# A two-block transformer forward pass on one NeuronCore: another order of weight splits, sums and solver steps within the long middle stage

## The chip, the cores and the metric

One NeuronCore of a Trainium2 chip runs the whole program. The metric is device microseconds from start to end of one execution. The engines are called as the profile calls them: PE (TensorE), PEld (its weight loads), DVE (VectorE), ACT (ScalarE), POOL (GpSimd) and SP (SyncE, which only issues DMAs here).

## What is computed

512 tokens of width 1024 go through two blocks in float32. Cut to what matters here:

```python
# first block, after its attention
x = x + merged @ w_o
u = relu(rmsnorm(x, g_mlp) @ w_up)                       # 1024 -> 4096
x = x + (u * u) @ w_down                                 # 4096 -> 1024
x = x + sigmoid(rmsnorm(x, g_ple) @ w_ple_gate) * (p @ w_ple)
x = rmsnorm(x, g_final)
# second block, first layer: gated delta rule
proj = rms_norm(x, pre_mix_norm) @ gdn_w_in              # q, k, v, z, b, a
q, k, v = silu(causal_conv4(proj[qkv]))                  # q and k then L2-normalised
z = proj[z]
# per chunk of tokens and head: a unit lower triangular system is solved
o = gated_delta_rule(q, k, v, g, beta)
x = x + rms_norm((rms_norm(o) * silu(z)) @ gdn_w_out)
```

Feed-forward layers, a forgetting attention and the first block's two attentions stand around this and are not touched.

## The kernel before

**Products.** Activations are kept with features on the partitions, `x[128, 8, 512]`. A float32 product is made of three passes of PE: each operand is split into a high part (rounded to fp32r) and a low part (what is left), and `product` issues high x high, high x low and low x high (lines 422 to 424). A tile of 128 output features over 1024 inputs is 8 steps k of 3 matmuls of 128x128 on 512 columns, 24 matmuls (`whole_tile`).

**Weights.** They come as a sequence of numbered chunks of up to 128x2048 (1 MB), in two slots used in turn. Chunk n is loaded by SP (line 192) once the low part of chunk n-2 is made; ACT writes its high part (`split_high`, line 213) once PE has finished with chunk n-2, since it overwrites that slot; DVE (`split_low_vector`, line 240) or POOL (`split_low`, line 230) then writes the low part, and PE waits for that. For most chunks this is two output tiles, 48 matmuls. Each engine goes through its own list in program order, so a split stands behind all that its engine was given before.

**The long stage.** `gdn_project` opens a stage without a barrier inside. Every engine first runs the parts of `Ahead` (merge, output projection of the attention, MLP, embedding, embedding gate), then its own part of the projection `gdn_in`:

- `Mlp` goes in two halves: 16 tiles up (8 chunks), ReLU on ACT, square on DVE, split; then 8 chunks down into 8 PSUM banks. DVE scales each bank by the norm's factor and adds it to x (`scale`, `add`). The norm's factor is not needed before that: sums of squares (`sum_squares`, line 1202), mean and reciprocal on DVE, `spread_factor` (line 1209) on PE, `copy_factor` (line 1219) on ACT.
- `PleGate`: chunks g0 to g3 of the gate, two tiles each. Per tile t DVE multiplies by the factor (line 1599), ACT takes tanh, DVE gates (line 1607) and adds to x (line 1610); then ACT and DVE split x for the next projection (`first_high`, `first_low`, line 1650) and square and accumulate it (lines 1658, 1668 and, with a gain, 1673). `FinalEntry.sum_squares` (line 1679) waits for all of these.
- The projection: chunk c0 works on the unnormalised split of x, with the sums in between; c1 is a narrow chunk of 16 columns; from c2 on `FinalEntry.operand` has made the normalised `split` (lines 1736 and 1740). The low parts of chunks c1 to c9 are made by POOL, the later ones by DVE. Each of the 24 tiles of q, k and v goes through a convolution: one tap and tanh on ACT (lines 2305, 2312), three taps on DVE from PSUM (line 2468), a product (line 2475). PE may reuse a bank when the taps have read it (`bank_free`).
- Side computations run beside it: masks and decays, and for the solver the blocks of a triangular matrix go out to DRAM and back as M and X (line 2176). `solve(j)`, 31 steps of two DVE instructions each (lines 2400, 2403), forms the inverse in X; it is copied transposed (line 2509) and both are written out.
- The gates z: two sides of 512 columns, two chunks each (z0 to z3). PE needs the banks read by DVE (line 2487) before the next side; line 2492 makes `z2`. In the kernel before, five solver steps follow each of the eight gate tiles.

The stage ends in a barrier of all engines (line 150), behind which `gdn_chain` starts at line 2579.

Of the kernel before, what the change touches and what calls it, by code (L numbers as in the profile page):

```python
# [4 lines left out]
P = 128  # L5
# [368 lines left out]
def build_program(nc, w, plan, constants, tables, out):  # L374
# [24 lines left out]
    with ctx:  # L399
# [953 lines left out]
        class Mlp:  # L1353
# [74 lines left out]
            def scalar(self, act):  # L1428
                self.entry.copy_factor(act)
                for half in range(2):  # L1430
                    for i in range(self.half_tiles):
                        n = self.half_tiles * half + i
                        act.wait_ge(weights.products, self.up_done(half, i))
# [5 lines left out]
                        if i % 2:  # L1439
                            weights.split_high(act, Chunk(self.up_chunk(half, i // 2) + 2))  # L1440
# [14 lines left out]
            def vector(self, dve):  # L1455
# [15 lines left out]
                dve.wait_ge(self.entry.factor_ready, 1)  # L1471
                for half in range(2):
                    for i in range(self.half_tiles):
# [68 lines left out]
        class PleGate:  # L1542
# [13 lines left out]
            def tensor(self, pe):  # L1556
                bank = Mlp.out_bank
                pe.wait_ge(self.embedding.read, 2)
                self.entry.first_chunks(pe, self.start, bank[0:2])
                pe.wait_ge(self.embedding.read, DT)  # L1560
                self.entry.sum_squares(pe)
                for t in range(2, DT):
# [5 lines left out]
                    if t == 2:  # L1568
                        self.entry.spread_factor(pe)

            def scalar(self, act):
# [4 lines left out]
                self.entry.copy_factor(act)  # L1576
                for t in range(DT + 1):
# [5 lines left out]
                    if t >= 1:  # L1583
# [3 lines left out]
                    if t % 2 and t < DT:  # L1587
                        weights.split_high(act, Chunk(self.start + t // 2 + 2))

            def vector(self, dve):  # L1590
# [4 lines left out]
                for t in range(DT):  # L1595
                    dve.wait_ge(weights.products, self.tiles0 + t + 1)
                    if t >= 2:
                        dve.wait_ge(self.tanh_ready, t - 1)
                    nc.vector.tensor_tensor(out=self.pre[:, t % 2, :], in0=psum[:, Mlp.out_bank[t % 4], :], in1=self.entry.factor[:],
                                            op=ALU.mult).then_inc(self.read, 1)  # L1600
                    if t >= 1:
                        self.following.first_low(dve, t - 1)
                        self.following.accumulate(dve, t - 1)
                    if t % 2 and t < DT - 1:
                        weights.split_low_vector(dve, self.start + t // 2 + 2)
                    dve.wait_ge(self.tanh_ready, t + 1)
                    nc.vector.scalar_tensor_tensor(out=self.gated[:, t % 2, :], in0=self.tanh[:, t % 2, :], scalar=1.0,
                                                   in1=self.embedding.kept[:, t, :], op0=ALU.add, op1=ALU.mult).then_inc(self.gated_ready, 1)
                    dve.wait_ge(self.gated_ready, t + 1)
                    nc.vector.tensor_tensor(out=x[:, t, :], in0=x[:, t, :], in1=self.gated[:, t % 2, :], op=ALU.add).then_inc(self.added, 1)  # L1610
                self.following.first_low(dve, DT - 1)
                self.following.accumulate(dve, DT - 1)
# [474 lines left out]
        def gdn_project(ahead_of, split, qkv, z2, lower, columns, scratch, kept, spare):  # L2087
# [19 lines left out]
            with stage("gdn_in", 133) as s:  # L2107
# [35 lines left out]
                with nc.Block() as block:  # L2143
                    @block.sync
                    def _(sp_):
# [32 lines left out]
                        weights.load(sp_, start + 15)  # L2178
                        sp_.wait_ge(col_dve, 17)
# [1099 lines left out]
```

## Time and profile before

| | |
|---|---|
| median of 3 runs | 2427.6 us (2426.79 to 2427.78) |
| the profiled execution, its own time | 2430.54 us |
| its span, first to last instruction | 2428.8 us |
| PE busy | 2238.0 us, 92% of the span |
| DVE, ACT, POOL busy | 1128.3, 811.1, 138.3 us |
| mean granted clock of PE | 0.955 |

Busy times of a pipelined PE are modelled; what counts is when its instructions start and what each waited for. Times in the rows are us from the start of the span.

### The profile page before, as it was taken

How to read it: one execution, taken by the hardware profiler on the slowest of the kernel's cores; microseconds unless marked ns; L12 is line 12 of the kernel's file. 1: busy time of each engine (PE TensorE's matmuls, PEld its weight loads, DVE VectorE, ACT ScalarE, POOL GpSimd, SP SyncE). 2: the span in 40 equal slices, each digit the busy share in tenths (PEclk: the TensorE clock that was granted, in tenths of full speed). 3: DMA queues.
4: the chain of work that ended last, by engine and by line, in shares of the span. 5: the costliest groups of instructions: out<-in, count | busy, mean ns of one | idle time of the engine just before them, and what ended most of it. 6: DMA issues, size and time to landing. Idle time of an engine off the chain costs nothing. (4 is left out here: it accounts for less than half of the span.)

```text
span 2428.8 us, 26752 instructions
## 1 busy us (share of the span) xinstructions
PE 2238.0 (92%) x10932; PEld 1765.1 (73%) x10932; DVE 1128.3 (46%) x1668; ACT 811.1 (33%) x1147; POOL 138.3 (6%) x52
## 2 busy tenths in 40 slices
PE   6998899989999997999597899999899898999997
PEld 4885467868878875787495688888678566888885
DVE  2014765633254266876564544431552545544413
ACT  4311374333133154443133332221332653322211
POOL 3331000000000001310010000000000000000000
PEclk9997899999999998999688999999999999999998
DMA  3311002222223222232202223222234012222321
GB/s 126 104 57 53 1 1 70 96 81 93 99 75 105 87 70 72 72 109 92 65 23 70 69 87 104 87 95 96 69 105 156 1 53 70 89 102 87 104 87 52
DMA packets 43015, 190.22 MB, mean 78 GB/s; under 512 B 15808, under 2 KB 16512, under 8 KB 22032
## 3 DMA queue, kind: packets, MB, share of 16 engines
q1 hardware_dynamic: 40560, 184.32, 22.2%
q10 hardware_dynamic: 2336, 4.23, 0.5%
q8 instruction: 85, 1.39, 0.2%
q14 instruction: 34, 0.28, 0.0%
HBM read 184.80 MB, written 3.74 MB: 78 GB/s over the span
## 5 line engine op out<-in xcount | busy, mean ns | idle before, releaser
L422 PE MATMUL psum<-split,weights_high 128*128 128x512 f32 x1688 | 680.6, 403 | 54.1 <-DVE split L1160 19.5
L424 PE MATMUL psum<-split,weights_low 128*128 128x512 f32 x1688 | 676.1, 401 | 0.0
L423 PE MATMUL psum<-split,weights_high 128*128 128x512 f32 x1688 | 674.1, 399 | 0.0
L240 DVE TENSOR_TENSOR weights_low<-weights_raw,weights_high 128x2048 fp32r<-128x2048 f32 x139 | 318.6, 2292 | 563.9 <-ACT weights_high L213 563.8
L213 ACT CAST weights_high<-weights_raw 128x2048 fp32r<-128x2048 f32 x164 | 309.8, 1889 | 588.7 <-PE psum L424 580.9
L422 PEld LDWEIGHTS psum<-split,weights_high 128*128 128x128 f32 x1688 | 321.8, 191 | 139.7 <-issue 26.0
L423 PEld LDWEIGHTS psum<-split,weights_high 128*128 128x128 f32 x1688 | 322.0, 191 | 77.9
L424 PEld LDWEIGHTS psum<-split,weights_low 128*128 128x128 f32 x1688 | 321.1, 190 | 79.0 <-issue 0.2
L230 POOL TENSOR_TENSOR weights_low<-weights_raw,weights_high 128x2048 fp32r<-128x2048 f32 (+3 forms) x25 | 108.2, 4329 | 862.4 <-ACT weights_high L213 855.3
L424 PE MATMUL psum<-hidden,weights_low 128*128 128x512 f32 x352 | 140.4, 399 | 0.0
L423 PE MATMUL psum<-hidden,weights_high 128*128 128x512 f32 x352 | 138.7, 394 | 0.0
L422 PE MATMUL psum<-hidden,weights_high 128*128 128x512 f32 x352 | 138.0, 392 | 0.0
L423 PE MATMUL psum<-hidden_low,weights_high 128*128 128x512 f32 x256 | 102.1, 399 | 0.0
L422 PE MATMUL psum<-hidden_high,weights_high 128*128 128x512 f32 x256 | 100.9, 394 | 0.0
L424 PE MATMUL psum<-hidden_high,weights_low 128*128 128x512 f32 x256 | 100.3, 392 | 0.0
L423 PEld LDWEIGHTS psum<-hidden,weights_high 128*128 128x128 f32 x352 | 66.1, 188 | 17.2
L422 PEld LDWEIGHTS psum<-hidden,weights_high 128*128 128x128 f32 x352 | 66.1, 188 | 15.8
L424 PEld LDWEIGHTS psum<-hidden,weights_low 128*128 128x128 f32 x352 | 66.1, 188 | 15.1
L1826 POOL TENSOR_TENSOR x_stream<-x_stream,ring 128x512 f32<-128x512 f32 x4 | 5.1, 1264 | 1148.8 <-DVE ring L1857 1145.0
L422 PE MATMUL psum<-weights_high,split 128*128 128x512 f32 (+1 forms) x164 | 63.8, 389 | 5.5 <-DVE weights_low L240 3.0
L2027 ACT ACTIVATE ring<-ring 128x512 f32<-128x512 f32 x44 | 27.9, 633 | 121.1 <-DVE ring L2053 121.1
L2468 DVE SCALAR_TENSOR_TENSOR gdn_spare<-psum,conv,gdn_spare 128x511 f32<-128x511 f32 (+2 forms) x72 | 53.8, 748 | 21.1 <-ACT gdn_spare L2305 19.4
(406 smaller groups left out, 2703.2 us busy)
## 6 DMA issues: line engine op xcount, KB each, us to landing
weights_raw<-in_weights SPq DMA_DIRECT2D x161, 1024.0 KB, 4.8
minus_c<-minus_c_rows ACTq DMA_DIRECT2D x16, 256.0 KB, 7.5
x_stream<-in_x SPq DMA_DIRECT2D x2, 1024.0 KB, 7.9
gdn_in_grown<-gdn_rows SPq DMA_DIRECT2D x4, 512.0 KB, 4.5
gdn_chain_grown<-gdn_rows SPq DMA_DIRECT2D x4, 512.0 KB, 4.1
out<-x_stream SPq DMA_DIRECT2D x8, 256.0 KB, 2.1
rope_table<-rope_tables SPq DMA_DIRECT2D x1, 1024.0 KB, 5.3
weights_raw<-in_weights SPq DMA_DIRECT2D x1, 768.0 KB, 4.2
```

The costliest lines, as they stand in the source:

```text
L213: self.nc.scalar.copy(self.high[:, chunk.slot, 0:width], self.raw[:, chunk.slot, 0:width]).then_inc(self.high_ready, 1)
L230: self.nc.gpsimd.tensor_tensor(out=self.low[:, chunk.slot, 0:width], in0=self.raw[:, chunk.slot, 0:width], in1=self.high[:, chunk.slot, 0: ...
L240: self.nc.vector.tensor_tensor(out=self.low[:, n % 2, 0:width], in0=self.raw[:, n % 2, 0:width], in1=self.high[:, n % 2, 0:width].bitcast( ...
L422: nc.tensor.matmul(bank, wh, ah, start=first, stop=False)
L423: nc.tensor.matmul(bank, wh, al, start=False, stop=False)
L424: return nc.tensor.matmul(bank, wl, ah, start=False, stop=last)
L1826: nc.gpsimd.tensor_tensor(out=x[:, m, :], in0=x[:, m, :], in1=self.scaled[:, m % 4, :], op=ALU.add).then_inc(self.odd_added, 1)
L2027: nc.scalar.activation(self.tanh[:, f % 2, :], self.gate[:, f % 2, :], ACT.Tanh, scale=0.5).then_inc(self.tanh_ready, 1)
L2468: nc.vector.scalar_tensor_tensor(out=mixed[:, o % 2, back:T], in0=psum[:, o % 4, 0:T - back], scalar=conv[:, at:at + 1], in1=mixed[:, o % ...
```

## The change

No instruction's work is changed. Weight splits, sums, spreads, solver steps and one load move to other places in the engines' lists, and the gate's additions, accumulations and splits on DVE stand one tile later against its multiplications by the factor.

```diff
@@ Mlp.scalar
-                self.entry.copy_factor(act)
+                weights.split_high(act, Chunk(self.start + 2))
                 for half in range(2):
                     for i in range(self.half_tiles):
                         n = self.half_tiles * half + i
+                        if n == 4:
+                            self.entry.copy_factor(act)
...
-                        if i % 2:
+                        if i % 2 and n > 1:
                             weights.split_high(act, Chunk(self.up_chunk(half, i // 2) + 2))
@@ Mlp.vector
-                dve.wait_ge(self.entry.factor_ready, 1)
+                weights.split_low_vector(dve, self.start + 2)
...
-                        if i % 2:
+                        if i % 2 and n > 1:
                             weights.split_low_vector(dve, self.up_chunk(half, i // 2) + 2)
...
-                    for c in range(self.half_chunks):
-                        if half == 0 or c < self.half_chunks - 1:
-                            weights.split_low_vector(dve, self.down_chunk(half, c) + 2)
+                    for c in range(self.half_chunks - 1):
+                        weights.split_low_vector(dve, self.down_chunk(half, c) + 2)
                     if half == 0:
+                        dve.wait_ge(self.entry.factor_ready, 1)
                         for m in range(DT):
                             scale(0, m)
                             add(0, m)
+                        weights.split_low_vector(dve, self.down_chunk(0, self.half_chunks - 1) + 2)
@@ PleGate.tensor
-                self.entry.first_chunks(pe, self.start, bank[0:2])
-                pe.wait_ge(self.embedding.read, DT)
-                self.entry.sum_squares(pe)
...
+                    if k == 5:
+                        pe.wait_ge(self.embedding.read, DT)
+                        self.entry.sum_squares(pe)
+                self.entry.spread_factor(pe)
...
-                    if t == 2:
-                        self.entry.spread_factor(pe)
@@ PleGate.scalar
                 self.entry.copy_factor(act)
+                weights.split_high(act, Chunk(self.start + 2))
                 for t in range(DT + 1):
...
-                    if t >= 1:
+                    if 1 <= t < DT:
...
-                    if t % 2 and t < DT:
+                    if t % 2 and 1 < t < DT:
                         weights.split_high(act, Chunk(self.start + t // 2 + 2))
+                act.wait_ge(self.added, DT)
+                self.following.square(act, DT - 1)
+                self.following.first_high(act, DT - 1)
@@ gdn_project, sync
                         weights.load(sp_, start + 15)
+                        weights.load(sp_, start + 16)
                         sp_.wait_ge(col_dve, 17)
@@ gdn_project, tensor
-                            if k == 4:
+                            if k == 3:
                                 entry.sum_squares(pe)
-                        entry.spread_factors(pe)
+                            if k == 5:
+                                entry.spread_factors(pe)
...
-                        pe.wait_ge(col_dve, 16)
-                        nc.tensor.transpose(psum[0:NH, 5, 3 * P:4 * P], R2, identity).then_inc(col_pe, 1)
...
+                                if side == half == 0:
+                                    pe.wait_ge(col_dve, 16)
+                                    nc.tensor.transpose(psum[0:NH, 5, 3 * P:4 * P], R2, identity).then_inc(col_pe, 1)
@@ gdn_project, scalar
-                        weights.split_high(act, Chunk(start + 2))
                         entry.copy_factor(act)
                         for t in range(DT):
                             entry.high(act, t)
-                            if t == 3:
-                                weights.split_high(act, Chunk(start + 3))
+                            if t == 2:
+                                weights.split_high(act, Chunk(start + 2))
                         entry.copy_residual_factor(act)
+                        weights.split_high(act, Chunk(start + 3))
...
                         for side in range(2):
+                            weights.split_high(act, Chunk(z_chunk + 2 + 2 * side))
                             for j in range(TT):
...
-                                if j == 0:
-                                    weights.split_high(act, Chunk(z_chunk + 2 + 2 * side))
@@ gdn_project, vector
+                        for step in range(14):
+                            solve(step)
                         for side in range(2):
+                            weights.split_low_vector(dve, z_chunk + 2 + 2 * side)
...
-                                for _ in range(5):
-                                    solve(done)
-                                    done += 1
-                            weights.split_low_vector(dve, z_chunk + 3 + side)
-                        while done < SOLVE - 1:
-                            solve(done)
-                            done += 1
-                        dve.wait_ge(taken, SOLVE - 1)
-                        nc.vector.tensor_copy(step_product, X.rearrange("p i c -> p c i")).then_inc(made, 1)
+                            if side == 0:
+                                weights.split_low_vector(dve, z_chunk + 3)
+                                for step in range(14, SOLVE - 1):
+                                    solve(step)
+                                dve.wait_ge(taken, SOLVE - 1)
+                                nc.vector.tensor_copy(step_product, X.rearrange("p i c -> p c i")).then_inc(made, 1)
```

In `PleGate.vector` the loop over t now runs to DT + 2. Iteration t multiplies tile t by the factor, gates and adds tile t - 1, and accumulates and splits tile t - 2; the low part of g2 stands in iteration 0 behind the first multiplication, that of g3 in iteration 3 and that of c0 in iteration 5.

DVE at the start of the embedding gate before (`ple_rings` holds the multiplied and gated tiles, `embedded` the embedding):

```order
L1599 TENSOR_TENSOR ple_rings<-psum,ple_factor 128x512
L1607 SCALAR_TENSOR_TENSOR ple_rings<-ple_rings,embedded 128x512
L1610 TENSOR_TENSOR x_stream<-x_stream,ple_rings 128x512
L1599 TENSOR_TENSOR ple_rings<-psum,ple_factor 128x512
L1650 SCALAR_TENSOR_TENSOR first_split<-x_stream,gdn_in_both_gains,first_split 128x512
L240 TENSOR_TENSOR weights_low<-weights_raw,weights_high 128x2048
L1607 SCALAR_TENSOR_TENSOR ple_rings<-ple_rings,embedded 128x512
L1610 TENSOR_TENSOR x_stream<-x_stream,ple_rings 128x512
L1599 TENSOR_TENSOR ple_rings<-psum,ple_factor 128x512
L1650 SCALAR_TENSOR_TENSOR first_split<-x_stream,gdn_in_both_gains,first_split 128x512
```

And in the changed kernel:

```order
L1616 TENSOR_TENSOR ple_rings<-psum,ple_factor 128x512
L240 TENSOR_TENSOR weights_low<-weights_raw,weights_high 128x2048
L1616 TENSOR_TENSOR ple_rings<-psum,ple_factor 128x512
L1624 SCALAR_TENSOR_TENSOR ple_rings<-ple_rings,embedded 128x512
L1628 TENSOR_TENSOR x_stream<-x_stream,ple_rings 128x512
L1616 TENSOR_TENSOR ple_rings<-psum,ple_factor 128x512
L1624 SCALAR_TENSOR_TENSOR ple_rings<-ple_rings,embedded 128x512
L1628 TENSOR_TENSOR x_stream<-x_stream,ple_rings 128x512
L1672 SCALAR_TENSOR_TENSOR first_split<-x_stream,gdn_in_both_gains,first_split 128x512
L1616 TENSOR_TENSOR ple_rings<-psum,ple_factor 128x512
L1624 SCALAR_TENSOR_TENSOR ple_rings<-ple_rings,embedded 128x512
L1628 TENSOR_TENSOR x_stream<-x_stream,ple_rings 128x512
```

The first weight split moves from behind the first tile's addition to behind its multiplication, and each tile's gating stands behind the next tile's multiplication.

DVE where the gates z begin, before, from the split of z1 on:

```order
L240 TENSOR_TENSOR weights_low<-weights_raw,weights_high 128x2048
L2487 SCALAR_TENSOR_TENSOR gdn_spare<-psum,gdn_in_gate_gain 128x512
L2492 SCALAR_TENSOR_TENSOR gdn_z<-gdn_spare 128x512
L240 TENSOR_TENSOR weights_low<-weights_raw,weights_high 128x2048
L2497 COPY gdn_in_rows_sb<-psum 32x128
L2499 TENSOR_SCALAR gdn_kept_columns<-gdn_kept_columns 128x32
L2500 TENSOR_SCALAR gdn_kept_columns<-gdn_kept_columns 128x32
L2400 TENSOR_TENSOR gdn_scratch<-gdn_scratch 128x31
L2403 TENSOR_TENSOR gdn_scratch<-gdn_scratch 128x31
```

And in the changed kernel, first the rows behind that split, then those from the end of the first 14 solver steps on:

```order
L2499 SCALAR_TENSOR_TENSOR gdn_qkv<-gdn_spare 128x512
L240 TENSOR_TENSOR weights_low<-weights_raw,weights_high 128x2048
L2424 TENSOR_TENSOR gdn_scratch<-gdn_scratch 128x31
L2427 TENSOR_TENSOR gdn_scratch<-gdn_scratch 128x31
L2424 TENSOR_TENSOR gdn_scratch<-gdn_scratch 128x30x2
```

```order
L2427 TENSOR_TENSOR gdn_scratch<-gdn_scratch 128x18x14
L240 TENSOR_TENSOR weights_low<-weights_raw,weights_high 128x2048
L2512 COPY gdn_in_rows_sb<-psum 32x128
L2514 TENSOR_SCALAR gdn_kept_columns<-gdn_kept_columns 128x32
L2515 TENSOR_SCALAR gdn_kept_columns<-gdn_kept_columns 128x32
L2520 SCALAR_TENSOR_TENSOR gdn_spare<-psum,gdn_in_gate_gain 128x512
L2525 SCALAR_TENSOR_TENSOR gdn_z<-gdn_spare 128x512
L2520 SCALAR_TENSOR_TENSOR gdn_spare<-psum,gdn_in_gate_gain 128x512
L2525 SCALAR_TENSOR_TENSOR gdn_z<-gdn_spare 128x512
```

The solver steps leave the gaps between the gate tiles: 14 stand ahead of the split of z2, the other 17 behind side 0.

## Rows read from the trace of the kernel before

**Rows 1.** Windows: length, busy per engine (instructions), granted clock, DMA share, GB/s.
```profile
540.00:600.00 60.00, 60.00 (x259) 48.27 (x258) 24.86 (x22) 19.84 (x22) 0.00 (x0) 1.00 0.28 95
```

**Rows 2.** Waits of PE over the whole run: total us, times, longest.
```profile
PE psum L422 <- DVE weights_low L240: 21.7, 6, 8.7
```

**Rows 3.** Timeline, start of the MLP: start, us, engine, line [idle before <-releaser].
```profile
502.17 1.05 PE L1209 MATMUL psum<-const,gdn_in_mlp_entry_stat 128*128 128x128 f32 x8
503.26 0.59 ACT L1219 COPY mlp_factor<-psum 128x512 f32<-128x512 f32 x1 [20.40 <-PE psum L1209]
511.95 0.80 PE L422 MATMUL psum<-split,weights_high 128*128 128x512 f32 x1 [8.73 <-DVE weights_low L240]
517.80 0.40 PE L424 MATMUL psum<-split,weights_low 128*128 128x512 f32 x1
```

**Rows 4.** Timeline, between the halves of the MLP.
```profile
671.10 0.39 PE L424 MATMUL psum<-hidden_high,weights_low 128*128 128x512 f32 x1
671.58 1.90 ACT L213 CAST weights_high<-weights_raw 128x2048 fp32r<-128x2048 f32 x1 [9.29 <-PE psum L424]
673.51 2.29 DVE L240 TENSOR_TENSOR weights_low<-weights_raw,weights_high 128x2048 fp32r<-128x2048 f32 x1 [8.89 <-ACT weights_high L213]
681.57 0.39 PE L422 MATMUL psum<-split,weights_high 128*128 128x512 f32 x1
```

**Rows 5.** Timeline, embedding gate, and a window of two of its tiles (columns as rows 1).
```profile
880.52 0.95 PE L1202 MATMUL psum<-const,square_sum 128*128 128x1 f32 x8
888.10 0.59 ACT L1219 COPY ple_factor<-psum 128x512 f32<-128x512 f32 x1 [6.20 <-PE psum L1209]
899.26 0.80 PE L422 MATMUL psum<-split,weights_high 128*128 128x512 f32 x1 [5.58 <-DVE weights_low L240]
...
905.65:919.32 13.67, 13.21 (x57) 10.33 (x56) 9.99 (x15) 6.56 (x9) 0.00 (x0) 1.00 0.08 20
```

**Rows 6.** Timeline, from the gate into the projection.
```profile
926.59 0.50 PE L422 MATMUL psum<-first_split,weights_high 128*128 128x512 f32 x1 [2.20 <-DVE weights_low L240]
940.71 1.87 PE L1679 MATMUL psum<-const,square_sum 128*128 128x1 f32 x8 [5.31 <-DVE square_sum L1668]
952.03 0.57 ACT L1722 COPY gdn_scratch<-psum 128x512 f32<-128x512 f32 x1
952.64 5.40 DVE L1736 SCALAR_TENSOR_TENSOR gdn_scratch<-x_stream,gdn_in_both_gains,gdn_scratch 128x512 f32<-128x512 f32 x2 [7.08 <-ACT gdn_scratch L1722]
```

**Rows 7.** Timeline, a split on POOL and what DVE does beside it.
```profile
990.12 4.61 POOL L230 TENSOR_TENSOR weights_low<-weights_raw,weights_high 128x2048 fp32r<-128x2048 f32 x1 [6.42 <-ACT weights_high L213]
990.52 0.18 DVE L2412 TENSOR_SCALAR gdn_in_raw<-psum 128x32 f32<-128x32 f32 x1
990.83 3.99 DVE L2416 SCALAR_TENSOR_TENSOR gdn_in_raw<-gdn_in_raw 128x64 f32<-128x64 f32 x1
```

**Rows 8.** Timeline, PE at its first tile that waits for a freed bank.
```profile
976.10 0.47 PE L422 MATMUL psum<-split,weights_high 128*128 128x512 f32 x1
```

**Rows 9.** Timeline, the gate sides z and the end of the stage.
```profile
1104.91 0.34 SPq L2176 DMA_DIRECT2D gdn_scratch<-gdn_blocks  x1
1117.35 0.40 PE L424 MATMUL psum<-split,weights_low 128*128 128x512 f32 x1
1137.57 0.69 DVE L2487 SCALAR_TENSOR_TENSOR gdn_spare<-psum,gdn_in_gate_gain 128x512 f32<-128x512 f32 x1 [12.44 <-ACT gdn_spare L2345]
1184.51 1.02 DVE L2509 COPY gdn_scratch<-gdn_scratch 128x1024 f32<-128x1024 f32 x1
1187.58 1.94 PE L2579 MATMUL psum<-const,gdn_qkv 128*128 128x128 f32 x8 [9.87 <-PEq L150]
```

**Rows 10.** Lines of DVE from 1141 to 1186: the inverse.
```profile
L2403 DVE TENSOR_TENSOR gdn_scratch<-gdn_scratch 128x31 f32<-128x31 f32 (+15 forms) x31 | 10.7, 344 | 1.1
L2400 DVE TENSOR_TENSOR gdn_scratch<-gdn_scratch 128x31 f32<-128x31 f32 (+15 forms) x31 | 10.6, 342 | 0.8
```

**Rows 11.** DMA issues: KB each, us to landing.
```profile
gdn_scratch<-gdn_blocks SPq DMA_DIRECT2D x1, 512.0 KB, 6.1
```

More of the change, by code:

```diff
@@ L1558, in tensor @@
                 pe.wait_ge(self.embedding.read, 2)
-                self.entry.first_chunks(pe, self.start, bank[0:2])
-                pe.wait_ge(self.embedding.read, DT)
-                self.entry.sum_squares(pe)
+                pe.wait_ge(weights.low_ready, self.start + 1)
+                high, low = weights.parts(Chunk(self.start), DT)
+                for k in range(DT):
+                    pe.wait_ge(self.entry.low_done, k + 1)
+                    for m in range(2):
+                        sl = slice(m * P, (m + 1) * P)
+                        last = product(psum[:, bank[m], :], (high[:, k, sl], low[:, k, sl]),
+                                       (self.entry.split[:, 0, k, :], self.entry.split[:, 1, k, :]), k == 0, k == DT - 1)
+                        if k == DT - 1:
+                            last.then_inc(weights.products, 1)
+                    if k == 5:
+                        pe.wait_ge(self.embedding.read, DT)
+                        self.entry.sum_squares(pe)
+                self.entry.spread_factor(pe)
                 for t in range(2, DT):
@@ L1611, in vector @@
-                self.following.first_low(dve, DT - 1)
-                self.following.accumulate(dve, DT - 1)
+                for t in range(DT + 2):
+                    if t < DT:
+                        dve.wait_ge(weights.products, self.tiles0 + t + 1)
+                        if t >= 2:
+                            dve.wait_ge(self.tanh_ready, t - 1)
+                        nc.vector.tensor_tensor(out=self.pre[:, t % 2, :], in0=psum[:, Mlp.out_bank[t % 4], :], in1=self.entry.factor[:],
+                                                op=ALU.mult).then_inc(self.read, 1)
+                    if t == 0:
+                        weights.split_low_vector(dve, self.start + 2)
+                    if 1 <= t <= DT:
+                        dve.wait_ge(self.tanh_ready, t)
+                        if t >= 3:
+                            dve.wait_ge(self.added, t - 2)
+                        nc.vector.scalar_tensor_tensor(out=self.gated[:, (t - 1) % 2, :], in0=self.tanh[:, (t - 1) % 2, :], scalar=1.0,
+                                                       in1=self.embedding.kept[:, t - 1, :], op0=ALU.add,
+                                                       op1=ALU.mult).then_inc(self.gated_ready, 1)
+                        dve.wait_ge(self.gated_ready, t)
+                        nc.vector.tensor_tensor(out=x[:, t - 1, :], in0=x[:, t - 1, :], in1=self.gated[:, (t - 1) % 2, :],
+                                                op=ALU.add).then_inc(self.added, 1)
+                    if t >= 2:
+                        self.following.accumulate(dve, t - 2)
+                        self.following.first_low(dve, t - 2)
+                    if t % 2 and 1 < t < DT - 1:
+                        weights.split_low_vector(dve, self.start + t // 2 + 2)
@@ L2178, in _ @@
                         weights.load(sp_, start + 15)
+                        weights.load(sp_, start + 16)
                         sp_.wait_ge(col_dve, 17)
                         sp_.dma_start(to_rows[1], rows_sb[:, 1, :]).then_inc(written, 16)
-                        for n in range(start + 16, weights.end("gdn_in") + 2):
+                        for n in range(start + 17, weights.end("gdn_in") + 2):
                             weights.load(sp_, n)
```

27 lines of the change are left out of this document (6 added, 21 removed).

## The prediction

> **What bounds the kernel now.** I read the page first (PE busy 92% of the span), then the waits of PE, then PE's timeline in the stage that the diff touches, and from each long gap the timelines of ACT and DVE back to what held them. Where nothing is late PE issues a 512-column matmul every 0.233 us (259 in 60 us, granted clock 1.00, its 2.4 GHz level [rows 1]), so a tile of 24 takes 5.6 us and a chunk of 48 takes 11.2. The reader is to see that the largest named wait is for low parts of weights, 21.7 us in six waits [rows 2], and that these low parts are late for reasons of order. Each gap also costs a restart: after the one in rows 3, 14 intervals last 5.85 us (511.95 to 517.80), 0.42 each, the 1.2 GHz level for most of them, where 3.3 would do. So I price each place by the first matmul that is issued the same way before and after, and never by the wait alone.
>
> **A. Start of the MLP.** PE finishes chunk 1 at 502.2 and stands until 511.95, because ACT made the high part of chunk 2 only behind the factor's copy, for which it waited 20.40 us [rows 3], and behind two ReLU tiles. Now the high part follows chunk 0's last matmul (at about 490, that is 502.17 less 11.2 for chunk 1 and 0.9 for the sums between) at the delays of rows 4: 0.48 us to ACT, 1.93 to DVE, 2.29 for the low part. It is ready near 495, wanted at 503. The factor's copy at tile 4 costs nothing: nobody reads the factor before the down part. ReLU 0 and 1 start 0.6 and 2 us late against their own data; they are not wanted before bank reuse at tile 6. Chunk 3, split after tile 3, is ready near 509 and wanted at 514. With no wait the 15th matmul stands at 502.17 + 0.9 (the spread and its restart; its row's 1.05 us contains a drain) + 14 x 0.233 = 506.3 in place of 517.80: **11.5 us**.
>
> **B. Between the halves.** PE ends at 671.10, ACT splits from 671.58, DVE from 673.51, and only then scales the bank that PE wants [rows 4]. Now the eight scale-and-add pairs run before that split. Their sixteen operations, at the 0.64 us or so that a 512-column step of DVE takes in rows 5 ((9.99 - 2.29) / 12), fit beside the last down chunk (11.2 us) but for its last tile; the split ends near 677.5 and its chunk is wanted at 682.5. The 13th matmul moves from 681.57 to 671.10 + 13 x 0.233 = 674.1: **7.4 us**.
>
> **C. Embedding gate and entry of the projection.** In before's times:
> - The sums move 12 matmuls ahead of 880.52 [rows 5], to 877.7, where the accumulation has long ended; the spread stands behind k = 7 instead of one tile later, so the factor's copy moves from 888.10 to 882.5. ACT and DVE then split g2 (1.9 + 2.3 us) by 887.3; PE wants it at 893.4. The wait of 5.58 us at 899.26 goes.
> - A round of two tiles takes DVE 9.99 us of work, the chunk's split included, and took 13.67 [rows 5] because DVE stood waiting for ACT. With gating one tile late these waits mostly fall under other steps, and PE's round is 11.2. So PE should run the gate's eight tiles without a stop: from 869.3 (48 matmuls before 880.52), 192 matmuls and two small sets of 0.9, to 915.9. By steps of 0.62 to 0.72 us, c0's low part comes at 913.5, 2.4 us early. c0 began at 926.59 [rows 6].
> - What is late next are the sums. PE reaches them after k = 3, at 921.5. DVE's last gate multiplication starts at 917.3 and twelve steps of some 0.64 us follow before the last accumulation; the sums start near 925.0, in place of 940.71 [rows 6]. PE waits 3.5 us here instead of 5.3, with one k fewer done, and restarts at the lower level again.
> - Sums 3.5, k = 4 and 5 at mixed clock 4.5, spread and its way to ACT 1.1: the factor is copied at 934.1. Before it was 952.03, behind a weight split on ACT [rows 6].
> - c2's split now starts after the third high part; POOL has it from 940.1 to 944.7. POOL takes 4.61 us for one and DVE is locked out meanwhile when it reads two operands from SBUF: an instruction of 64 columns took 3.99 us beside it, while one from PSUM took 0.18 [rows 7]. Before, the same lock hit the first operand steps (5.40 us for two [rows 6]); so it is moved, not added. PE has done k = 6, 7, c1 and the residual spread by 943.0, waits 1.8 us, and ends c2 at 956.5 (11.2 us and 0.5 for the restart).
> - c3's split on ACT follows the residual factor's copy at 949.7, POOL has it from 951.7 to 956.3. PE's first tile that waits for a bank starts at 956.8, before 976.10 [rows 8]: **19.3 us**. From there both orders are the same until the last tile of v.
>
> One rule matters in that last step. The taps of tile 0 fall into POOL's split, and they read PSUM and one SBUF operand. If they were locked out too, they would end at 956.3 + 2.3 and C would give 17.6 us. By the 0.18 us row they are not. The Trainium skill (SBUF — State Buffer, Who interferes with whom) says that a DVE instruction with at most one SBUF input does not contend with GpSimd and one with two does. By that rule rows 7 read as they stand, and C keeps its 19.3.
>
> **D. Gates z, solver, barrier.** The last tile of v ends at 1117.6 [rows 9]. Transposing R2 no longer stands before z0, so z0 ends at 1128.8. DVE is free at 1137.57 - 12.44 = 1125.1, and M has been there since 1104.91 + 6.1 [rows 9, 11]. All 31 solver steps take 10.7 + 10.6 + 1.9 = 23.2 us [rows 10]; the first 14 are 10.3 of it by their starts in the timeline (31 to 252 elements per partition, 0.49 to 0.91 us), so they end at 1135.4. z2's high part is made beside them, its low part is ready at 1137.7, wanted at 1140.4. Side 0's four gate tiles, two steps each, end at 1143.4 and free the banks in time. z3's load no longer queues on SP behind a wait for DVE; its low part is ready at 1145.7, wanted at 1151.6. PE ends side 1 at 1162.8. On DVE follow 17 steps (12.9, to 1158.6), the copy (1.02), one weight split (to 1162.0) and four gate tiles, each second one waiting for tanh: end near 1167.4. Before, DVE ended at 1184.51 + 1.02 = 1185.53 and PE went on behind the barrier 2.05 later [rows 9]. POOL's clearing, which began 0.6 later still because the inverse was just being written, can now start at once: **18.7 us**. The chain itself is the same.
>
> **Sum.** 11.5 + 7.4 + 19.3 + 18.7 = 56.9 us. The profiled execution's own time is 2430.54 (span 2428.8), so it becomes 2373.6; the median of the runs is 2.9 lower, and gives **2370.7 us**. Bounds: each of the four could lose its last 1 to 2 us to waits below my steps; and the two stops of PE inside the convolution could shrink by some us, since DVE has slightly more lead. I take 50 to 64 us as this case's own range.
>
> **Rivals.**
> 1. DVE becomes the bound of the gate. Its 9.99 us of 11.2 leave 1.2 per round for every wait for ACT, and before the waits were 3.7. If the round stays at 13.67, three rounds come 7.4 us later; c0's low part is late by 5.0, and sums and factor move by 7.4. Gain 49.5, time 2378. Against it: tanh is always issued a tile before it is read.
> 2. The end does not follow: z2 or the banks late because 14 solver steps stand before them (slack 2.7 us), or the barrier's way out bound by PE. If D gives only what PE itself gains, 1187.58 - 9.87 - 1162.8 = 14.9 less a restart, 13 us, and loses a 4 us stop at z2, the gain is 38.2 + 9 = 47, time 2381.
> 3. Slower: PE's clock. 57 us are paid back if PE, now without its pauses, gets the 1.2 GHz level in runs of matmuls: each costs 0.42 - 0.233 = 0.19 us more, so from 300 matmuls on, of some 2,700 between 490 and 1190, it is slower; with 500 of them the time is 2370.7 + 0.19 x 500 = 2466. Against it: 259 matmuls in a row at 1.00 [rows 1]; the lower level follows pauses only.
> 4. The change does not do what it says: each moved split is held by another condition of the same list (the slot still read, the load not in). Then nothing moves, 2427. Against it: the chunk's slot was free at each moved place by the rows.
>
> **Numbers.** Forecast 0.68, rival 1 0.17, rival 2 0.10, rival 3 0.03, rival 4 0.02. A measurement of this kernel tells 0.2% (5 us) from no change. The range from 2362 to 2388 holds the forecast's own (2364 to 2378), rivals 1 and 2 and some us of a third stop. Faster 0.95, same 0.02, slower 0.03.
>
> **What would show it.** A: no gap of PE over 1 us before the seam of the halves; B: none there. C: c0 starts within 1 us of the end of g3; the sums 3 to 4 us after PE's last k = 3; one short wait for POOL at c2. D: no wait from the last tile of v to the barrier, solver steps in two blocks, DVE last. Wrong would be a PE wait for DVE's lines 1616 or 1628 inside the gate, or of over 2 us at z2, and a granted clock under 1.00 in the MLP.

## The result and the profile after

| | before | changed |
|---|---|---|
| median | 2427.69 us (4 runs, 2426.79 to 2429.9) | 2371.02 us (4 runs, 2367.97 to 2372.5) |
| the profiled execution, its own time (span) | 2430.54 us (2428.8) | 2372.2 us (2370.2) |
| mean granted clock of PE | 0.955 | 0.964 |

The ratio is 0.9763, 95% interval [0.9748, 0.9777]: 57 us faster, where 2370.7 us was forecast. That the medians agree to 0.3 us is luck to that digit: run again, the same kernel had a median of 2367.2 (experiment 2).

All waits of PE in the changed kernel from the embedding gate to the last tiles, 858 to 1115 (total us, times, longest):

```profile
PE psum L1701 <- DVE square_sum L1690: 3.4, 1, 3.4
PE psum L2281 <- DVE gdn_in_work L2451: 1.9, 1, 1.9
PE psum L422 <- POOL weights_low L230: 1.4, 1, 1.4
PE psum L2219 <- ACT gdn_in_squares L2345: 1.2, 1, 1.2
PE psum L2219 <- ACT gdn_in_decay L2345: 0.7, 1, 0.7
```

No wait for a low part made by VectorE is left here [rows 2]. The second line was there before with the same 1.9 us; the last is new.

Windows of the changed kernel (columns as [rows 1]): the start of the MLP, the seam of its halves, the gate and the entry of the projection, the end of the stage.

```profile
480.00:520.00 40.00, 40.00 (x182) 32.52 (x181) 19.25 (x23) 16.05 (x19) 0.00 (x0) 1.00 0.24 79
...
665.00:685.00 20.00, 20.00 (x88) 16.08 (x87) 8.91 (x9) 6.45 (x9) 0.00 (x0) 1.00 0.31 106
...
870.00:957.00 87.00, 82.26 (x376) 64.57 (x376) 71.96 (x93) 45.55 (x63) 19.06 (x5) 0.98 0.24 79
...
1100.00:1130.00 30.00, 24.16 (x104) 19.26 (x103) 26.24 (x51) 7.25 (x8) 0.81 (x1) 0.95 0.28 102
```

In the first two, PE is busy without a gap at a granted clock of 1.00; there stood the pauses of [rows 3] and [rows 4]. In the last, VectorE is busy for 26.2 of 30 us; PE's last matmul starts at 1123.00 and VectorE's last instruction at 1126.96, so PE is not what holds the end.

PE's timeline in the changed kernel, in order the places of [rows 6], [rows 8] and [rows 9]:

```profile
906.96 1.05 PE L1701 MATMUL psum<-const,square_sum 128*128 128x1 f32 x8 [3.38 <-DVE square_sum L1690]
907.87 1.23 PE L1704 MATMUL psum<-const,gdn_scratch 128*128 128x1 f32 x8
936.62 0.50 PE L422 MATMUL psum<-split,weights_high 128*128 128x512 f32 x1
1129.23 1.94 PE L2602 MATMUL psum<-const,gdn_qkv 128*128 128x128 f32 x8 [5.84 <-PEq L150]
```

**Cutting the gain into the four places.** The stretch ahead of the MLP takes some us more or less from execution to execution, although its instructions are the same (the spread of the MLP's factor stood at 502.17 before, 502.95 here, 499.2 in other runs below), so I measure from that spread on: A to PE's last matmul of the first half, B from there to its 13th after it, C on to the transposed rows ahead of tile 4 of the projection (0.56 us ahead of 976.10 before), D on to PE's first matmul of the chain.

| part | forecast | before | changed | gain |
|---|---|---|---|---|
| A, start of the MLP | 11.5 | 168.93 | 157.47 | 11.5 |
| B, seam of the halves | 7.4 | 10.47 | 3.04 | 7.4 |
| C, gate and entry | 19.3 | 293.97 | 272.81 | 21.2 |
| D, tiles, gates z, barrier | 18.7 | 212.04 | 192.96 | 19.1 |
| sum | 56.9 | 685.41 | 626.28 | 59.1 |

C is off its term by 1.9 us; the runs say where that arises. D looks closer than it is: its 18.7 held 0.6 us for POOL's clearing, which lies behind the point where D ends here. That term is right (POOL started 0.64 us after PE's first matmul of the chain before, 0.04 us ahead of it now), but like for like D is 18.1 forecast and 19.1 measured.

### The profile page after: what moved, and what is told of

It reads as the page before. It is cut to its first block and busy times, and to the rows that moved or that the text cites. A ratio compares the mean times of both kernels' runs of the same rounds, so it can differ in the third digit from the quotient of the medians.

```text
span 2370.2 us, 26758 instructions
## 1 busy us (share of the span) xinstructions
PE 2222.4 (94%) x10932; PEld 1755.5 (74%) x10932; DVE 1125.2 (47%) x1668; ACT 811.6 (34%) x1147; POOL 137.9 (6%) x52
```

## The experiments

Ratios are to the kernel before, with 95% intervals, from three rounds, or from five where effects of 2 to 5 us were expected.

**1. Each part alone, on the kernel before.** The diffs are those of the change, cut by place: the hunks of `Mlp` without those on the last down chunk (A), those on it (B), `PleGate` and the entry's sums, spreads and splits (C), the load, the transposition, the splits of z and the solver (D).

```diff
@@ A (with its counterpart on DVE)
-                self.entry.copy_factor(act)
+                weights.split_high(act, Chunk(self.start + 2))
@@ B
                     if half == 0:
                         for m in range(DT):
                             scale(0, m)
                             add(0, m)
+                        weights.split_low_vector(dve, self.down_chunk(0, self.half_chunks - 1) + 2)
```

> The kernel before with part A alone (split of the MLP's chunk 2 ahead of the factor's copy). My theory, the four places add: PE's gap of 9.8 us behind the spread is gone and the gaps between the halves (5.4 us), in the gate (6.0) and at the sums (5.7) stand as before; 11.5 us less, ratio 0.9953. Rival, the places hide behind each other (loads or DVE's lead make up for the lost pause at a later gap): a later gap grows and the gain is 6 us or less, ratio 0.9975 or more.

> The kernel before with part B alone (scaling and adding ahead of the split of the last down chunk). Theory of adding places: only the gap between the halves goes, with its restart at 0.43 us a matmul: 7.4 us less, ratio 0.9969. Rival: only the wait itself (5.1 us) comes back, because the lower clock has another cause: ratio 0.9979.

> The kernel before with part C alone (embedding gate one tile late, its splits and sums moved, entry of the projection). Theory: 21.4 us, as the two traces show between PE's 13th matmul of the second half and its first tile that waits for a bank (my forecast for it was 19.3): ratio 0.9912. Rival: 19.3 us belong to C and the other 2 came from A and B through loads that are further ahead: ratio 0.9920, and the sums start 5 us or so behind k = 3.

> The kernel before with part D alone (gates z, solver steps in two blocks, one load). Theory: DVE bounds the end on both sides, so the whole move comes through: 18.9 us less, ratio 0.9922, z2's low part before PE wants it, no PE wait from the last tile of v to the barrier. Rival: without C the solver's blocks come in later against PE (they depend on loads and DMAs, not on PE), DVE waits for M, and the gain is 15 us or less: ratio 0.9938 or more.

| alone | ratio | from the spread to the chain | gain of it in that trace |
|---|---|---|---|
| A | 0.9955 [0.9938, 0.9973] | 675.22 | 10.2 |
| B | 0.9978 [0.9968, 0.9989] | 677.45 | 8.0 |
| C | 0.9913 [0.9891, 0.9936] | 665.80 | 19.6 |
| D | 0.9916 [0.9895, 0.9937] | 666.49 | 18.9 |

The places add: the four ratios multiply to 0.9764, the change has 0.9763, and the four gains make 56.7 us. In the trace of A alone every later pause is still there: 5.06 us at the seam, 5.58 in the gate and 3.63 at c3, as before, and 6.85 at the sums, where it was 5.31. So one later wait did grow, by 1.5 us, as the rival had it, but 10.2 of the 11.5 us came through. B alone lies between its two theories by time (3.9 us by the medians, interval 2.7 to 7.8), and on the side of 7.4 by its trace, in which the 13th matmul behind the seam comes 3.03 us after it in place of 10.47. I take the trace, since the pause and its restart are both gone there, but the times don't confirm the full 7.4.

C alone gained 19.6, close to my term. Its own stretch was 275.33, a gain of 18.6. So the 21.4 that I expected of it did not come, and neither did the sign of the rival, a wait of 5 us at the sums. By time the two can't be told apart. PE's rows at its sums show what differs from the changed kernel, behind the same wait:

```profile
922.28 1.87 PE L1698 MATMUL psum<-const,square_sum 128*128 128x1 f32 x8 [3.38 <-DVE square_sum L1687]
924.01 1.84 PE L1701 MATMUL psum<-const,gdn_scratch 128*128 128x1 f32 x8
```

Here the two sets took 1.73 and 1.71 us from start to start; in the changed kernel 0.91 and 1.09.

**2. The changed kernel once more, unchanged.**

> The changed kernel once more, unchanged, for one thing: its trace lacks the lower clock at the sums (two sets of eight in 0.91 and 1.09 us behind a wait of 3.4), while part C alone, with the same wait, took 1.73 and 1.71. Theory: how soon the lower clock comes behind the same pause differs from execution to execution, so this trace shows another restart, 1 to 2 us dearer, and part C comes out nearer to 19.3 than to 21.4. Rival: the restart belongs to the program, the same rows come back within 0.1 us, and the 2 us are a real gain that I missed.

Measured: 0.9752 [0.9735, 0.9768], median 2367.18 us. The same place in the trace of this run:

```profile
903.21 1.15 PE L1701 MATMUL psum<-const,square_sum 128*128 128x1 f32 x8 [3.37 <-DVE square_sum L1690]
904.23 1.85 PE L1704 MATMUL psum<-const,gdn_scratch 128*128 128x1 f32 x8
905.93 0.78 PE L422 MATMUL psum<-first_split,weights_high 128*128 128x512 f32 x1
```

The wait is the same to 0.01 us, the second set costs 1.70 in place of 1.09, and C comes out 1.6 us longer (274.36, a gain of 19.6). From spread to chain it is 628.55, 56.9 us less than before: to the tenth the forecast sum, which is luck to that digit. So the same program pays a different restart behind the same pause from execution to execution, as my theory said. The granted clock over the sixteen matmuls of the two sets was 0.90 in the first trace of the changed kernel, 0.65 in this one and 0.50 in that of C alone. The Trainium skill (TensorE: Matmul & The Clock Gate, Part 1) says of the rise to the faster clock that its point varies from run to run. These three traces show such a variation where the clock falls: 0.91 and 1.09, 1.02 and 1.70, 1.73 and 1.71 us for the same sixteen matmuls.

Of the two traces the first is the odd one. `tail_split` and `grown_first` (experiment 6) run the same instructions up to tile 4, and their C is 274.47 and 274.40, a gain of 19.5 and 19.6. The kernel before has a spread of its own: the same stretch took 293.97 in its trace and 293.96 to 295.21 in those of A, B and D alone.

**3. Rival 1: the gate's additions back in their own tile.**

```diff
-                for t in range(DT + 2):
+                for t in range(DT):
...
+                    dve.wait_ge(self.tanh_ready, t + 1)
+                    nc.vector.scalar_tensor_tensor(out=self.gated[:, t % 2, :], ...
```

> The changed kernel with the gate's additions back in their own tile (splits and sums stay moved). Theory: the delay is what keeps DVE ahead; without it a round of two tiles takes 13.67 us again as in rows 5, PE waits inside the gate for DVE, c0 is 5 us late and the sums move by 7.4: 2378 us, ratio to before 0.9796. Rival: the early split of g2 and the factor 5.6 us earlier give DVE enough lead by themselves, and the delay is worth nothing: 2371, ratio 0.9766, no wait of PE for ple_rings.

Measured: 0.9807 [0.9792, 0.9822], 2380.46 us. The delay is worth some 10 us (11 and 13 by the ratios of the two measurements of the changed kernel, 9.8 to 11.5 by the traces at tile 4). VectorE's waits in the gate (858 to 913) of this kernel, then of the changed one:

```profile
DVE square_sum L1686 <- ACT gdn_scratch L1676: 11.7, 7, 1.8
DVE ple_rings L1615 <- ACT ple_factor L1219: 3.8, 1, 3.8
DVE weights_low L240 <- ACT weights_high L213: 2.0, 3, 1.1
```

```profile
DVE weights_low L240 <- ACT weights_high L213: 7.8, 4, 3.0
DVE ple_rings L1616 <- ACT ple_factor L1219: 3.8, 1, 3.8
DVE ple_rings L1616 <- PE psum L424: 2.0, 1, 2.0
```

Without the delay each tile costs a wait of 1.83 us for ScalarE's squares of the tile just added. Its timeline shows what a round then takes:

```profile
883.91 0.68 DVE L1615 TENSOR_TENSOR ple_rings<-psum,ple_factor 128x512 f32<-128x512 f32 x1
...
889.64 0.68 DVE L1615 TENSOR_TENSOR ple_rings<-psum,ple_factor 128x512 f32<-128x512 f32 x1
...
898.10 0.68 DVE L1615 TENSOR_TENSOR ple_rings<-psum,ple_factor 128x512 f32<-128x512 f32 x1
```

Two tiles take 14.2 us (883.91 to 898.10) against PE's 11.2, so three rounds fall 9 us behind, and the sums come 413.03 us after the spread instead of 404.01. In the changed kernel VectorE waits for PE once in the gate: it is ahead. Two points of my rival were off. It is not tanh but the squares that VectorE waits for; they stand behind the next tile's tanh on ScalarE, which itself waits 3.4 to 4.3 us for VectorE's multiplication. And PE hardly stops inside the gate (0.65 us for a low part, no wait for `ple_rings`): four banks take up the lag, and it is paid at c0 (2.7 us) and at the sums (8.5 us).

**4. What the wait at the sums is worth.**

```diff
-                            if k == 3:
+                            if k == 5:
                                 entry.sum_squares(pe)
-                            if k == 5:
-                                entry.spread_factors(pe)
+                        entry.spread_factors(pe)
```

> The changed kernel with the sums behind k = 5 and the spread behind k = 7. PE does 12 more matmuls (2.8 us) before the sums, so its wait of 3.4 us for the accumulation should shrink to 0.6. Theory: nothing is gained, because c2 waits for its low part on POOL (924.9 in the changed kernel), which hangs on the factor, and the factor comes no earlier: the wait moves from the sums to c2, within 1 us of 2371, ratio 0.9766. Rival: the wait at the sums is on the path, and 2 to 3 us come back: 2368.5, ratio 0.9756.

Measured: 0.976 [0.9745, 0.9775], 2369.27 us. The wait at the sums is gone and stands at c2:

```profile
921.72 0.80 PE L422 MATMUL psum<-split,weights_high 128*128 128x512 f32 x1 [4.11 <-POOL weights_low L230]
```

4.1 us in place of 1.4, as the theory said. By time the two theories are within each other's interval, so the trace has to decide, and it shows the theory right in the place and wrong in a reason. Behind a wait of only 0.57 us the sums kept the faster clock, and the factor did come earlier: it was copied 409.8 us after the spread, against 411.4 in the first trace of the changed kernel and 412.9 in the repeated one. But the wait of 4.1 us at c2 then brought the lower clock there (granted 0.50, 0.43 us a matmul), so that tile 4 came at 433.88, against 433.32 and 434.87: at most 1 us gained. What ends last is the chain from factor to POOL's split.

**5. That split on VectorE.**

```diff
@@ operand, after the fifth product
+                        dve.wait_ge(weights.low_ready, weights.start["gdn_in"] + 2)
+                        weights.split_low_vector(dve, weights.start["gdn_in"] + 2)
@@ POOL
-                        for n in range(start + 1, vector_low_from):
+                        weights.split_low(pool, Chunk(start + 1))
+                        pool.wait_ge(weights.low_ready, start + 3)
+                        for n in range(start + 3, vector_low_from):
```

> The changed kernel with the low part of c2 made by VectorE (2.3 us) in place of POOL (4.6 us), in the middle of the operand's steps. Theory: POOL's split is both late and locks VectorE for 4.0 us; now c2 is ready at 922.5 in place of 924.8, VectorE is 1.7 us ahead, PE starts c2 2.3 us earlier: 2368.7, ratio 0.9757. Rival: PE then waits for the operand's low parts at each k, since VectorE is the bound there, and the time stays at 2371, ratio 0.9766.

> Both together and c2's high part directly behind the factor's copy. Theory: c2 is ready at 919.1, PE comes to it at about 920.2 from c1 and the residual spread, and the whole 4.6 us between that and 924.9 come back less the 1 us that the operand's first steps take: 2367, ratio 0.9750. Rival: the later high parts of the operand on ScalarE (1.9 us later) hold VectorE, and c2 starts where it did: 2371, ratio 0.9766.

The second kernel has both edits and moves the high part:

```diff
                         entry.copy_factor(act)
+                        weights.split_high(act, Chunk(start + 2))
                         for t in range(DT):
                             entry.high(act, t)
-                            if t == 2:
-                                weights.split_high(act, Chunk(start + 2))
```

Measured: 0.9751 [0.9737, 0.9764] for the first, 0.9731 [0.9718, 0.9744] (2362.59 us) for the second. The first can't be told from the changed kernel by time. In its trace no wait is left at c2, but the restart behind the sums was a dear one (2.8 us for the two sets, the factor copied at 412.9), so it has to be held against the repeated run, where the factor stood at 412.9 too. There PE started c2 423.5 us after the spread and tile 4 at 434.87; here it is 421.9 and 433.25, both 1.6 us earlier, with no wait for the operand's low parts. That is the theory's way and 0.7 us short of its 2.3. The second comes to tile 4 at 427.31, 6 to 7.6 us earlier and more than the 3.6 I had worked out, because PE now meets neither the pause at the sums and at c2 nor the lower clock. A new wait of 2.14 us for POOL stands at c3; the matmuls behind it start 0.23 us apart at once. Its rows at the sums:

```profile
905.09 1.05 PE L1701 MATMUL psum<-const,square_sum 128*128 128x1 f32 x8 [0.57 <-DVE square_sum L1690]
906.00 1.03 PE L1704 MATMUL psum<-const,gdn_scratch 128*128 128x1 f32 x8
906.90 0.48 PE L422 MATMUL psum<-first_split,weights_high 128*128 128x512 f32 x1
```

A wait of 0.57 us, 0.9 us per set, and the next products at 0.23 us at once. The factor is copied at 910.88, 409.8 after the spread against 411.4 (914.30) and 412.9 in the two traces of the changed kernel.

**6. The end of the stage, and what stands behind it.** `tail_split` takes the last low split out of VectorE's list in front of side 1's gate tiles and puts it at the head of the chain. `grown_first` lets the decay rows of the chain's chunk 0 go before the wait for the cleared inverse.

```diff
@@ tail_split
                         for side in range(2):
-                            weights.split_low_vector(dve, z_chunk + 2 + 2 * side)
                             if side == 0:
+                                weights.split_low_vector(dve, z_chunk + 2)
...
+                        weights.split_low_vector(dve, weights.end("gdn_in"))
                         difference(0)
@@ grown_first
                         sp.wait_ge(written, 48)
+                        sp.dma_start(grown[:]..., to_rows[1, 0:GH, :]...).then_inc(grown_in, 16)
                         sp.wait_ge(zeroed, 2)
```

> The changed kernel with the last low split of the stage (2.3 us, VectorE, in front of side 1's gate tiles) put behind the barrier, at the head of VectorE's part of the chain, where VectorE waits 14.9 us for a transfer. Theory: VectorE alone sets the end of the stage, so the four gate tiles start 2.2 us earlier, bound then by PE's last tiles (1123.4): 2368.8, ratio 0.9757. Rival: PE's last tile and its tanh bind already, the barrier moves by less than 0.7 us: 2370.5, ratio 0.9764.

> The changed kernel with the transfer of the decay rows for chunk 0 issued before the wait for the cleared inverse, ahead of the seven pieces of the inverse. It asks what the start of the chain hangs on, once the stage before it ends earlier. Theory: VectorE's differences (1142.6) and with them ScalarE's exponential stand in front of the copy that PE waits 5.3 us for; they end 8 us earlier, the copy follows PE directly at about 1141.3 and PE goes on 4 us earlier: 2366.9, ratio 0.9749. Rival: the pieces of the inverse, cleared by POOL until 1134.4, bind all that follows: within 1 us of 2371, ratio 0.9766.

`tail_split` measured 0.9752 [0.9738, 0.9765], which time alone can't tell from the changed kernel; its trace can. PE stands 4.04 us at the barrier instead of 6.23 (its last matmul at 1123.88, the first of the chain at 1127.92):

```profile
1127.92 2.29 DVE L240 TENSOR_TENSOR weights_low<-weights_raw,weights_high 128x2048 fp32r<-128x2048 f32 x1 [1.57 <-PEq L150]
```

That is the 2.2 us of the theory, and it shows once more that VectorE alone sets the end; the split itself now lies where VectorE has nothing to do. `grown_first` measured 0.9741 [0.9728, 0.9754], 2365.97 us. In the changed kernel, and then in this one:

```profile
1146.30 0.90 PE L2635 MATMUL psum<-gdn_chain_inverse_t,gdn_chain_y 32*32 32x32 f32 x13 [5.25 <-ACT gdn_chain_y L2787]
```

```profile
1141.47 0.89 PE L2635 MATMUL psum<-gdn_chain_inverse_t,gdn_chain_y 32*32 32x32 f32 x13
```

PE's L2625 starts at 1139.33 and 1139.96, so L2635 follows it by 6.97 us before and by 1.51 now. ScalarE's copy had stood behind an exponential, that behind VectorE's differences, and those behind one transfer queued after seven others. 5.5 us came back in the trace where 4 were expected. By the ratios it is 3 to 5 us, and the intervals overlap with those of the changed kernel.

**7. All of them.**

> All found orders in one: sums late, c2 ahead and on VectorE (ratio 0.9731 alone), the last split behind the barrier (2.2 us), the decay rows first (4 us), and half of the clearing on VectorE instead of POOL (POOL's 1.8 us of 5.3 on the path to the transfers). Theory: they add, 2362.6 - 2.2 - 4 - 1.8 = 2354.6, ratio 0.9698. Rival: the last three stand in one chain behind the barrier and share a gain of 4: 2358.6, ratio 0.9714.

Measured: 2355.56 us, ratio 0.9702 [0.9688, 0.9715], 12 to 15 us faster than the changed kernel by the ratios of its two measurements, and 73.6 faster than the kernel before of the same batch (2429.13). They add, within 1 us; the rival's 0.9714 is just inside the interval. The traces speak against it: behind `c2_ahead` 1.4 us were gained up to the chain's first matmul and 6.5 us from there to the product that waits for ScalarE's copy (10.18 us in place of 16.73), 7.9 together where 8.0 were expected. The divided clearing was not run alone. The clearing, one part on each engine at the same time:

```profile
1119.21 3.52 POOL L2771 MEMSET gdn_chain_inverse_t<- 128x4096 f32 x1 [111.87 <-POOLq L150]
```

```profile
1119.71 1.76 DVE L2940 MEMSET gdn_chain_inverse<- 128x2048 f32 x1 [2.03 <-PEq L150]
```

## Why the prediction was right

**A, right in mechanism and size.** 11.5 us forecast and found. The pause of 9.78 us is gone with its restart. The factor's copy at tile 4 cost nothing, as costed (granted clock 1.00 and PE busy without a gap from 503 to 858).

**B, right.** 7.4 in both traces of the changed kernel. Alone it could not be measured to better than 2.7 to 7.8 us.

**C, right but for a term that no trace fixes.** Counted from the 13th matmul behind the seam, as the prediction's times are (18.1 us to add), PE ended k = 3 at 921.5 as forecast, the sums started at 925.07 (925.0), POOL split c2 from 938.4 (940.1) and c3 from 949.7 (951.7), and the first tile that waits for a bank started at 954.7 (956.8). Of the 2.1 us at that tile 1.7 arise between the sums' start and the factor's copy. I had 9.1 us for this: 3.5 for the sums and 4.5 for k = 4 and 5, at the lower clock, and 1.1 for the spread. The first trace spent 7.3, part C alone 9.9, and the repeated run, `tail_split`, `grown_first` and `c2_vector` 8.9 each. So the term was not mis-sized by a fixed amount: it varies by 1.6 us between executions of the changed kernel, the forecast is near its usual value, and the repeated run's C gave 19.6.

The step that decided between 19.3 and 17.6 held. The three taps of the first tile fall into POOL's split of c3 and are not slowed, while the product behind them, with two operands from SBUF, is:

```profile
931.58 4.63 POOL L230 TENSOR_TENSOR weights_low<-weights_raw,weights_high 128x2048 fp32r<-128x2048 f32 x1 [6.76 <-ACT weights_high L213]
```

```profile
932.13 2.32 DVE L2492 SCALAR_TENSOR_TENSOR gdn_spare<-psum,conv,gdn_spare 128x511 f32<-128x511 f32 x3 [0.39 <-ACT gdn_spare L2330]
935.14 1.62 DVE L2499 SCALAR_TENSOR_TENSOR gdn_qkv<-gdn_spare 128x512 f32<-128x512 f32 x1 [0.70 <-ACT gdn_spare L2337]
```

Three taps in 2.32 us beside POOL (2.31 in the window without it, at 936.69), the product 1.62 instead of 0.69, until POOL's end at 936.2. The Trainium skill (SBUF — State Buffer, Who interferes with whom) draws this line between one and two operands from SBUF; the trace agrees.

**D, right, step by step.** With 39.4 us to add (PE's last sums of squares stood at 1105.49 and stand at 1066.06), the solver's blocks started at 1125.1 (1125.1 forecast) and 1145.4 (1145.7), the copy at 1158.5 (1158.6), the last split at 1159.5 to 1161.7 (1162.0), and VectorE ended at 1167.1 (1167.4). PE did not wait between the last tile of v and the barrier. In the order of these steps:

```profile
1085.63 0.21 DVE L2424 TENSOR_TENSOR gdn_scratch<-gdn_scratch 128x31 f32<-128x31 f32 x1
...
1105.96 0.42 DVE L2424 TENSOR_TENSOR gdn_scratch<-gdn_scratch 128x255 f32<-128x255 f32 x1
...
1119.02 1.12 DVE L2532 COPY gdn_scratch<-gdn_scratch 128x1024 f32<-128x1024 f32 x1
...
1126.96 0.69 DVE L2525 SCALAR_TENSOR_TENSOR gdn_z<-gdn_spare 128x512 f32<-128x512 f32 x1
```

Of the 1 us that D gained beyond its 18.1, half is the way out of the barrier: from VectorE's end to PE's first matmul 1.6 us, where I had kept the 2.05 of before. Why it is shorter is open.

**Rival 1** was a real danger: without the delay of the gate the time is 2380, and I had given it 2378 and 0.17 (7.4 us for three rounds of 13.67, which were 9 us for rounds of 14.2). My argument against it named the wrong data (tanh instead of the squares), though the change delays both. **Rival 2** did not come: z2 was never waited for. **Rival 3**: the granted clock in the MLP stayed at 1.00. **Rival 4** fell with the first trace. Of the two stops in the convolution one stayed (1.9 us) and one went from 1.7 to 1.2, while a new one of 0.7 came at the same line (not in the repeated run); that is part of D's stretch.

## What to carry to other kernels

Price a pause of PE by the first matmul that is issued the same way before and after, with its restart, and add such prices place by place: here four of them gave the sum to 0.1 us in one trace and 2.2 in another. Profile the same kernel more than once before you explain 1 or 2 us, and hold a variant against the trace that had the same restart (`c2_vector`). When a wait can be moved (sums, experiment 4), follow the chain that feeds the next one first; the gain comes only when that chain is shortened too, and then the lost restart comes on top. A barrier hides order mistakes on both of its sides: work of the engine that ends last belongs behind it when that engine then waits, and the transfer that a chain hangs on belongs at the head of its queue.

## What was not expected of the hardware

- Behind one and the same wait of 3.4 us, the way from the sums to the factor differed by 1.6 us between executions of one program (experiment 2), and behind the wait of 1.4 us at c2 there was no lower clock in the changed kernel.
- VectorE and POOL cleared two SBUF arrays at the same time, and POOL was not slowed: 3.52 us for 4096 elements per partition, as alone (3.51). VectorE took 1.76 for 2048; it was not measured alone.
- The stretch ahead of the MLP, whose instructions the change does not touch, took 498.2 to 502.95 us in these traces. PE's first matmul stands at 19.5 to 19.9 in all of them, so it is not the start of the trace that moves; most of the difference arises between 194 and 277 us. The stretch behind the chain's first matmul varied as much, 1236.9 to 1241.4, in the traces whose kernels leave it alone. A comparison of two profiled spans carries both; a count between two common instructions doesn't.
